# Attention's output projection in three fp32r passes, its weights through the split ring

## The reference, cut to what matters

```python
o = diff_attention(q, k, v, lam, rel_bias)            # 4 heads x 128
o = rms_norm(o, subln[l], SUBLN_EPS) * (1.0 - lam_init)
y_a = o.reshape(B, S, D_ATTN) * jax.nn.silu(z_a)      # 512 x 512
...
m = jax.nn.sigmoid(g_a) * (y_a @ w_pa[l]) + jax.nn.sigmoid(g_h) * (y_h @ w_ph[l])
x = x + rms_norm(m @ w_out[l], post_norm[l], NORM_EPS)
```

## Time and profile before

| | us |
|---|---|
| median of three runs | 2135.15 (2129.75 to 2135.77) |
| profiled execution | 2135.83 |
| its span | 2133.8 |
| TensorE busy, matmul rows | 2038.1 (96%) |
| VectorE / ScalarE / GpSimd busy | 1258.6 / 913.7 / 650.2 |
| mean granted TensorE clock | 0.972 |

### The profile page before, as it was taken

One profiled execution on the slowest core, in us unless ns is written; L12 is line 12 of the kernel. 1 busy time (PEld: TensorE's weight loads), 2 busy tenths in 40 slices (PEclk: granted clock), 3 DMA queues, 4 the chain that ended last, 5 costly groups with the idle time before them and its releaser, 6 DMA issues.

```text
span 2133.8 us, 28186 instructions
## 1 busy us (share of the span) xinstructions
PE 2038.1 (96%) x10992; PEld 1543.0 (72%) x10992; DVE 1258.6 (59%) x1994; ACT 913.7 (43%) x1458; POOL 650.2 (30%) x308
## 2 busy tenths in 40 slices
PE   8999999999999999999999998999999999989997
PEld 6667874657767775567777787777877878867776
DVE  4688945447779864465758844545134876464432
ACT  4432245333432345343357346446234743454531
POOL 2323431224324332033334212223433422222252
PEclk9999999998999999999899999899999999989998
DMA  6223221142322332132222001112332210111232
GB/s 226 84 92 116 93 90 52 68 138 79 113 99 72 107 104 69 50 119 69 104 89 80 28 27 43 50 52 93 104 117 86 89 48 15 35 60 50 66 108 84
DMA packets 47858, 174.26 MB, mean 82 GB/s; under 512 B 5646, under 2 KB 6286, under 8 KB 46320
## 3 DMA queue, kind: packets, MB, share of 16 engines
q1 hardware_dynamic: 47600, 172.34, 23.9%
q10 hardware_dynamic: 128, 0.13, 0.0%
HBM read 157.77 MB, written 14.68 MB: 81 GB/s over the span
## 4 chain that ended last, share of the span: by engine, by line
PE 73%; DVE 21%; ACT 3%; issue 2%; DMA 1%; DVEq 0%; ACTq 0%
PE bank L610 13%; PE bank L619 13%; PE bank L624 12%; PE bank L727 4%; PE bank L739 2%; PE bank L1152 2%; PE bank L1132 2%; PE bank L655 1%; PE bank L810 1%; PE bank L824 1%; PE bank L887 1%; DVE arena L1943 1%; DVE arena L1947 1%; PE bank L747 1%; DVE arena L1945 1%
## 5 line engine op out<-in xcount | busy, mean ns | idle before, releaser
L2497 POOL TENSOR_TENSOR w_lo<-wraw,w_hi 128x1024 fp32r<-128x1024 f32 (+2 forms) x248 | 591.8, 2388 | 1341.9 <-ACT w_hi L1222 1341.9
L1222 ACT ACTIVATE w_hi<-wraw 128x1024 fp32r<-128x1024 f32 (+2 forms) x248 | 253.1, 1021 | 690.2 <-PE bank L624 428.4
L610 PE MATMUL bank<-h_hi,w_hi 128*128 128x512 f32 x1568 | 409.7, 404 | 4.9 <-DVE arena L2231 3.8
L619 PE MATMUL bank<-h_lo,w_hi 128*128 128x512 f32 x1568 | 388.9, 390 | 0.2
L624 PE MATMUL bank<-h_hi,w_lo 128*128 128x512 f32 x1536 | 379.5, 389 | 0.0
L610 PEld LDWEIGHTS bank<-h_hi,w_hi 128*128 128x128 f32 x1568 | 294.1, 191 | 96.7 <-issue 31.8
L619 PEld LDWEIGHTS bank<-h_lo,w_hi 128*128 128x128 f32 x1568 | 294.7, 188 | 64.0 <-DVE h_lo L1782 1.6
L624 PEld LDWEIGHTS bank<-h_hi,w_lo 128*128 128x128 f32 x1536 | 288.3, 188 | 59.9
L727 PE MATMUL bank<-arena,wdir 128*128 128x512 f32 x256 | 114.7, 599 | 1.2 <-DMA wdir<-in_w_direct 1.2
L1979 DVE CUSTOM_DVE_ANT_0 arena<-bank,arena 128x512 f32<-128x512 f32 x64 | 44.3, 692 | 89.7 <-PE bank L810 88.4
L2403 DVE TENSOR_TENSOR bank<-bank,con 128x128 f32<-128x128 f32 x64 | 19.2, 300 | 129.4 <-PE bank L1138 128.3
(11 more groups left out here) (402 smaller groups left out, 3256.1 us busy)
## 6 DMA issues: line engine op xcount, KB each, us to landing
wraw<-in_w_split SPq DMA_DIRECT2D x220, 512.0 KB, 3.3
wdir<-in_w_direct SPq DMA_DIRECT2D x16, 512.0 KB, 3.3
x_park<-arena SPq DMA_DIRECT2D x3, 2048.0 KB, 6.3
arena<-x_park SPq DMA_DIRECT2D x3, 2048.0 KB, 7.8
wraw<-in_w_split SPq DMA_DIRECT2D x12, 384.0 KB, 3.0
hg_park<-arena SPq DMA_DIRECT2D x2, 2048.0 KB, 8.6
arena<-hg_park SPq DMA_DIRECT2D x2, 2048.0 KB, 7.9
wraw<-in_w_split SPq DMA_DIRECT2D x16, 256.0 KB, 2.6
```

What stands on the lines that cost most here:

```text
L610: mm(ps[0:wd, 0:S], hi[:, k, :].bitcast(F32R), h_hi[:, k, :].bitcast(F32R), start=k == 0 and not begun, stop=False)
L619: ins = mm(ps[0:wd, 0:S], hi[:, k, :].bitcast(F32R), h_lo[:, k, :].bitcast(F32R), start=False, stop=bool(parts) and k == KT - 1)
L1222: a(w_hi[:, n % 2, 0:f].bitcast(F32R), wraw[:, n % 2, 0:f], ACT.Copy).then_inc(hi_done, 1)
L2497: nc.gpsimd.tensor_tensor(w_lo[:, n % 2, 0:f].bitcast(F32R), wraw[:, n % 2, 0:f], w_hi[:, n % 2, 0:f], ALU.subtract).then_inc(lo_done, 1)
```

## The change

`pa` leaves the direct path. Its name goes into `PAIRED` with four parts, so each of its four chunks of a layer (two tiles each) goes through the ring ahead of `wo`'s. The code for such a tile, which stood in the second block, becomes a function `paired_tile` for both. y_a gets a leading part `za_hi` (ScalarE, `keep_leading`, one copy of 128 x 512 for each head) and a remainder `za_lo` (VectorE, `leave_rest`). TensorE's wait for the last head gives way to a wait for each part in the first `pa` tile. ScalarE makes the leading parts of the chunks two places ahead inside the loop that makes `h_hi`. The residual is loaded in four transfers of 512 KB, each behind a weight load. `wdir` is left to `ph`. TensorE then has 96 fp32r matmuls per layer in place of 32 in fp32.

The diff, cut to what the text speaks of:

```diff
@@ -56,7 +56,7 @@
 CHUNK = KT * P
 
 
-PAIRED = {"qr": 3, "qn": 3, "kn": 2, "vv": 2}
+PAIRED = {"pa": 4, "qr": 3, "qn": 3, "kn": 2, "vv": 2}
 SPLIT = ("u", "q", "k", "v", "za", "zh", "gh", "ga", "lx", "gc", "gba", "lz", "mq", "mkv", "gz", "mz",
          "wo", "wo2")
 PARTS = {"A0": 0, "M0": 1, "A1": 2, "M1": 3, "B0": 4, "V0": 5, "B1": 6, "V1": 7}
...
@@ -174,7 +174,7 @@
 
 
     split, direct = [], []
-    per = {"pa": 2, "ph": 2}
+    per = {"ph": 2}
     for job in psum_plan():
         g, l, n = job[0], job[1], job[-1]
         if g == "wo2":
...
@@ -196,9 +196,10 @@
     for n in range(len(direct)):
         todo.append((-5 if n < 2 else at[direct[n - 2][1]] + 0.2, "direct", n))
     for l in range(DEPTH):
+        todo += [(at["pa", l, 2 * n] + 0.3, "x in", f"A{l}{n}") for n in range(4)]
         todo += [(at["flt", l, 0, 3, 1] + 0.3, "filter weights", l), (at["u", l, 9] + 0.3, "park", l),
                  (at["iy", l, 0, 3] + 0.3, "unpark", l),
-                 (at["iy", l, 1, 3] + 0.3, "bias", l), (at["os", l, H - 1] + 0.3, "x in", f"A{l}"),
+                 (at["iy", l, 1, 3] + 0.3, "bias", l),
                  (at["ps", l] + 0.3, "x out", f"A{l}"), (at["mo", l, MH - 1] + 0.4, "x in", f"B{l}")]
         if l:
             todo += [(at["os", l - 1, H - 1] + 0.4, "layer", l), (at["wo2", l - 1, KT - 1] + 0.3, "x out", f"B{l - 1}")]
...
@@ -370,6 +375,10 @@
         lu, lr, li, la, lbb = (view(rb, n, 4, S) for n in ("lt", "XT", "X", "qg", "at"))
         lw = arena[:, rb["spare"]:rb["spare"] + 512].rearrange("p (g j c) -> p g j c", g=2, j=4)
         row_q = rs[:, :]
+        with early:
+            za_lo, za_hi = (typed(name, at, 4 * S)[:, :].rearrange("p (k s) -> p k s", k=4) for name, at in
+                                   (("za_lo", ra["za"]), ("za_hi", rt["WT"] + 4 * S)))
+        early_tiles[0], typed_to[0] = False, 0
         oa_rest = typed("oa_rest", rb["oa"], 4 * S).rearrange("p (h s) -> p h s", h=4)
         oc_rest = typed("oc_rest", rb["oc"], 4 * S).rearrange("p (h s) -> p h s", h=4)
         parts_at = typed("kr_parts", rb["mq"], 3 * S)
...
@@ -551,14 +560,17 @@
                 elif kind == "x in":
                     l = int(n[1])
                     if n[0] == "A":
+                        k = slice(2 * int(n[2]), 2 * int(n[2]) + 2)
                         sp.wait_ge(*after("ya", l, H - 1))
+                        if l:
+                            sp.wait_ge(x_out, 16 * l)
+                            sp.dma_start(xs["A1"][:, k, :], t["x_park"][:, k, :]).then_inc(x_in, 16)
+                        else:
+                            sp.dma_start(xs["A1"][:, k, :], t["xT"].rearrange("(k p) s -> p k s", p=P)[:, k, :]).then_inc(x_in, 16)
                     else:
                         sp.wait_ge(*full("mo", l, MH - 1))
-                    if n == "A0":
-                        sp.dma_start(xs["A1"], t["xT"].rearrange("(k p) s -> p k s", p=P)).then_inc(x_in, 16)
-                    else:
                         sp.wait_ge(x_out, 16 * NORMS[n])
-                        sp.dma_start(xs["B1"] if n[0] == "B" else xs[n], t["x_park"]).then_inc(x_in, 16)
+                        sp.dma_start(xs["B1"], t["x_park"]).then_inc(x_in, 16)
                 elif kind == "x out":
                     l = int(n[1])
                     if n[0] == "A":
...
@@ -625,6 +637,27 @@
                                  stop=k == KT - 1)
                 ins.then_inc(filled(*job), 1)
 
+            def paired_tile(g, l, j, src_hi, src_lo, made):
+
+                kt = PAIRED[g]
+                n = SPLIT_AT[g, l, j - j % 2]
+                hi, lo = (part[:, n % 2, 0:2 * kt * P].rearrange("p (j k n) -> p j k n", j=2, k=kt)[:, j % 2, :, :]
+                          for part in (w_hi, w_lo))
+                ps = take(g, l, j)
+                pe.wait_ge(hi_done, n + 1)
+                for k in range(kt):
+                    if made:
+                        pe.wait_ge(*after(f"{made}_hi", l, k))
+                    mm(ps[:, 0:S], hi[:, k, :].bitcast(F32R), src_hi[:, k, :].bitcast(F32R), start=k == 0, stop=False)
+                pe.wait_ge(lo_done, n + 1)
+                for k in range(kt):
+                    mm(ps[:, 0:S], lo[:, k, :].bitcast(F32R), src_hi[:, k, :].bitcast(F32R), start=False, stop=False)
+                for k in range(kt):
+                    if made:
+                        pe.wait_ge(*after(f"{made}_lo", l, k))
+                    ins = mm(ps[:, 0:S], hi[:, k, :].bitcast(F32R), src_lo[:, k, :].bitcast(F32R), start=False, stop=k == kt - 1)
+                ins.then_inc(filled(g, l, j), 1)
+
             def split_pair(first, second, parts):
 
                 n = SPLIT_AT[first]
...
@@ -720,7 +753,10 @@
                     if g in SPLIT:
                         split_tile(g, l, j)
                         return
-                    per, kt, src = {"pa": (2, 4, za), "ph": (2, 4, uc)}[g]
+                    if g == "pa":
+                        paired_tile(g, l, j, za_hi, za_lo, "za" if j == 0 else None)
+                        return
+                    per, kt, src = 2, 4, uc
                     ps = take(g, l, j)
                     w = direct_w((g, l, j - j % per), kt)
                     for k in range(kt):
...
@@ -846,7 +882,6 @@
                     column_sums(("os", l, h), [(tmp[:, h % 2, :], ("o_sq", l, h))])
                 for j in BEFORE_HEAD_NORM[H]:
                     tile("ga", j)
-                pe.wait_ge(*after("ya", l, H - 1))
                 for j in range(KT):
                     tile("pa", j)
                 for j in range(KT):
...
@@ -874,25 +909,8 @@
                     if g in SPLIT:
                         split_tile(*((g, l) if j is None else (g, l, j)))
                         return
-                    kt = PAIRED[g]
...
+                    paired_tile(g, l, j, src_hi, src_lo, made if j == 0 and g != "qn" else None)
...
@@ -1443,6 +1461,9 @@
                         for half in range(2):
                             gates_ = PH[:, 4 * half:4 * half + 4, :]
                             a(gates_, gates_, ACT.Sigmoid).then_inc(up("gh_sig", l, half), 1)
+                def keep_leading(h):
+                    a(za_hi[:, h, :].bitcast(F32R), za[:, h, :], ACT.Copy).then_inc(up("za_hi", l, h), 1)
+
                 keep("ga", 1)
                 keep_values(H - 1)
                 for h in range(H):
...
@@ -1456,12 +1477,21 @@
                     if h:
                         act.wait_ge(*after("ya", l, h - 1))
                     root(("os", l, h), P, EPS5)
+                    if h:
+                        keep_leading(h - 1)
                 for j in BEFORE_HEAD_NORM[H]:
                     keep("ga", j)
+                act.wait_ge(*after("ya", l, H - 1))
+                keep_leading(H - 1)
                 for half in range(2):
                     gates_ = PA[:, 4 * half:4 * half + 4, :]
                     a(gates_, gates_, ACT.Sigmoid).then_inc(up("ga_sig", l, half), 1)
-                parts_hi(f"M{l}", PA, lambda k: after("gated", l, k))
+
+                def gated(k):
+                    await_split("pa", l, k)
+                    return after("gated", l, k)
+
+                parts_hi(f"M{l}", PA, gated)
                 for j in range(KT):
                     if j == KT - 1:
                         load_roots()
...
@@ -2009,6 +2039,11 @@
                         dve.wait_ge(*full("ph", l, j))
                         dve.wait_ge(*after("gh_sig", l, j // 4))
                         v.tensor_tensor(PH[:, j, :], bank("ph", l, j)[:, 0:S], PH[:, j, :], ALU.mult).then_inc(release("ph", l, j), 1)
+                def leave_rest(h):
+                    dve.wait_ge(*after("za_hi", l, h))
+                    v.tensor_tensor(za_lo[:, h, :].bitcast(F32R), za[:, h, :], za_hi[:, h, :],
+                                    ALU.subtract).then_inc(up("za_lo", l, h), 1)
+
                 for h in range(H):
                     dve.wait_ge(*read("os", l, h))
                     dve.wait_ge(*read("za", l, h))
...
@@ -2017,6 +2052,9 @@
                                                     ALU.mult))
                     v.tensor_tensor(za[:, h, :], za[:, h, :], oA[:, h, :], ALU.mult).then_inc(up("ya", l, h), 1)
                     dve.wait_ge(*after("ya", l, h))
+                    if h:
+                        leave_rest(h - 1)
+                leave_rest(H - 1)
                 for j in range(KT):
                     dve.wait_ge(*full("pa", l, j))
                     dve.wait_ge(*after("ga_sig", l, j // 4))
...
@@ -2025,7 +2063,7 @@
                     dve.wait_ge(*read("ph", l, j))
                     v.tensor_tensor(PA[:, j, :], PA[:, j, :], PH[:, j, :], ALU.add).then_inc(up("gated", l, j), 1)
                 lo_odd(f"M{l}", PA)
-                dve.wait_ge(x_in, 16 * (l + 1))
+                dve.wait_ge(x_in, 64 * (l + 1))
                 for j in range(KT):
                     dve.wait_ge(*full("wo", l, j))
```

28 lines of the change are left out of this document (7 added, 21 removed).

## The result

| | before | after |
|---|---|---|
| median, 9 runs each | 2135.8 us (2129.75 to 2137.43) | 2141.12 us (2140.22 to 2141.66) |
| ratio, 95% interval | | 1.0024 [1.0015, 1.0033] |
| profiled execution, its span | 2135.83, 2133.8 | 2141.27, 2139.4 |
| mean granted clock of that execution | 0.972 | 0.968 |

The forecast was 2139.6 with a range of 2131 to 2146. The change costs a quarter of a per cent: a slowdown, but one inside the 0.3% that the prediction had called no change.

What follows compares the result with a forecast made beforehand. TensorE's own stream and its waits were taken as the bound. To the profiled 2135.83 it added 0.8 (layer 1 +1.1, layer 0 -0.35) and 3.6 for the clock, giving 2140.2; the median being 0.7 lower, 2139.6 us, range 2131 to 2146.

Steps and rivals of the forecast that it cites:

- F: When VectorE sees the last `pa` result, 0.27 us after `pa` leaves TensorE; put at T + 23.9.
- T: Start of `pa` on TensorE in each layer; 437.89 in layer 0 and 938.38 in layer 1 before the change.
- The passes and the start: In `pa`: fp32r passes gain 12.0 us over both layers; a first-tile wait for the last head costs 1.8 per layer.
- The ring: Weight chunks and residual during `pa`: no cost; layer 0's third chunk has 3.5 us cover, at worst costs 1.5.
- The first `wo` tile: GpSimd's four even remainders wait behind the second chunk's split, 1.71 us each; second `wo` tile starts at T + 34.9.
- The clock: Gaps between matmul pairs in the first `wo` tile halve TensorE's clock behind them: 1.8 us per layer, 3.6 in all.
- The sign, 0.50 in the tile behind: Evidence to look for: a granted clock of 0.50 in the tile behind the four waits for remainders.
- Rival A: The clock holds through the matmul pairs of the first `wo` tile; time 2136 us, chance 0.22.
- Rival C: The 1.8 us wait at the start of `pa` drops the clock too, 3.3 us per layer; 2146 us, chance 0.15.
- B: Rival: remainders in the first `wo` tile are not late, second tile at T + 29.9; 2126 us, chance 0.08.

Runs made afterwards that it cites:

- a2: Changed kernel, with ScalarE making the last head's leading part ahead of the last `ga` tile's two instructions; 2138.84 us, ratio 1.0012.
- a3: Changed kernel with the edits of a1 and a2 together; 2131.87 us, ratio 0.9975.
- c1: Changed kernel with a2's edit, and the gated sum's remainders on GpSimd and VectorE spread through `pa` instead of in a block; 2130.21 us, ratio 0.9962.
- c3: Changed kernel with a2's edit, and all eight gated-sum remainders on VectorE, GpSimd left with the weight splits; 2127.4 us, ratio 0.9962.
- c4: a3, with TensorE running the second `wo` tile's first pass between the first tile's second and third passes; 2125.16 us, ratio 0.9952.
- a1: Changed kernel, with GpSimd's four even remainders one chunk earlier, ahead of the split of the second `wo` chunk; 2132.14 us, ratio 0.9985.
- a5: Changed kernel, with VectorE's four odd remainders for `wo` cut from 512 to 8 columns, the rest left uncomputed; 2135.47 us, ratio 0.9999.
- a4: Changed kernel, with four needless matmuls ahead of each pair in the first `wo` tile's third pass, waits kept; 2137.31 us, ratio 1.0003.

## Why the prediction was right

The mechanism, each of its places and the size of each large term held; the size of the clock's term partly by luck. By its steps, from the profiled executions:

| step | predicted | measured |
|---|---|---|
| 96 matmuls of `pa` | 21.8 | 22.09 |
| wait in the first `pa` tile | 1.8 | 1.83 (942.98 - 940.47 - 0.68) |
| F | T + 23.9 | T + 24.12 (964.59) |
| split of the second `wo` chunk ends | F + 3.7 | F + 3.7 (968.26) |
| four even remainders end | F + 10.5 | F + 10.45 (975.04) |
| second `wo` tile, full clock | T + 34.9 | T + 35.1 |
| clock, both layers | 3.6 | 3.69 |
| everything else | 0 | +0.8 |

**The passes and the start.** Both right. An fp32r matmul took 0.230 in passes of four (22.09 / 96), a little over the 0.227 of the earlier trace rows. That is what made F 0.2 late; the 0.27 from the last matmul to VectorE stood in no row, and was 0.20 (964.39 to 964.59). The copy of the last head stood behind the two instructions named, as ScalarE's rows show:

```profile
940.72 1.06 ACT L1240 ACTIVATE w_hi<-wraw 128x1024 fp32r<-128x1024 f32 x1 [3.94 <-issue]
941.68 0.58 ACT L1322 ACTIVATE arena<-bank 128x512 f32<-128x512 f32 x1
942.29 0.63 ACT L1465 ACTIVATE za_hi<-arena 128x512 fp32r<-128x512 f32 x1
```

**The ring.** TensorE waited for no chunk, as said, but the reason given was wrong. The cover of 3.5 us for the third chunk in layer 0 was worked out with a landing of 3.3 us and without GpSimd's part of the split. The small loads of the next layer, some 1 MB, had gone out in the 4 us ahead of it, the chunk landed 6.0 us after its issue, and ScalarE waited 1.61 for it:

```profile
446.68 1.06 ACT L1240 ACTIVATE w_hi<-wraw 128x1024 fp32r<-128x1024 f32 x1 [1.61 <-DMA wraw<-in_w_split]
```

GpSimd then split it from 447.82 to 450.23, and TensorE's second pass of the fifth tile wanted that at 437.07 + 1.83 + 13 x 0.92 = 450.9. The cover was 0.7 us, and it existed only thanks to the 1.8 us at the start; a2, a3, c1, c3 and c4, which have no start wait, all wait there for 0.93 to 1.12. A median of a transfer is taken from a queue that is mostly quiet; behind a burst it isn't the number to use.

**The first `wo` tile.** Right in every part: the order of waits, 1.71 us for a remainder (four took 6.83) and GpSimd's turn coming first. a1 shows that GpSimd's order was the decisive wait, and a5 that 1.71 is 1.27 plus the hold-off. The Trainium skill, "SBUF — State Buffer", section "Who interferes with whom", says that a VectorE operation with at most one SBUF input, outside the two-port modes, stays out of the contention with GpSimd, and that one with two does not when GpSimd reads SBUF; c1's rows agree, 0.68 for the one and 2.18 for the other beside the same GpSimd instruction.

**The clock.** The two lengths at 0.50 that the earlier trace rows show, 3.3 and 6.7 us, both came: the longer in layer 0, the shorter in layer 1, each partly inside the waits, where it costs nothing. The cost of 3.6 was a choice between 3.4 and 6.8 that was not worked out, so it is partly luck that 3.69 was measured; a2's execution has the longer one in both layers. The sign, 0.50 in the tile behind, was too strong: the level was 0.50 for the first 3.4 us of the second tile in layer 0 and the first 1.8 in layer 1. Rival A, that the clock holds, is refuted by 0.76 and 0.85 over the second tiles; a4 shows that it is the gaps that do it. Rival C, that the wait of 1.8 us at the start drops the clock too, is refuted by 1.00 over the whole of `pa` in both layers. But its condition was not a good one, as the last section shows.

**B**, that the remainders are not late, is refuted by four waits. It is what c4 comes nearest to: with 2125.16 it reaches B's 2126, by an edit to TensorE's order.

The profiled execution came out 1.1 us above the sum (2141.27 against 2140.2). The start of the second tile accounts for 0.4 of that, the clock for 0.1, and the untouched stretches for the rest. The medians of the nine runs each are 5.3 apart, where the forecast says 4.4.

Three expectations of the experiments did worse than the prediction. a1, a3 and c1 were to be 4 to 7 us faster than they were, above all for one reason: I moved GpSimd's instructions and costed VectorE's at their undisturbed 0.69. The late third chunk in layer 0 (a3, c1) and the clock behind the waits that stayed are the rest. In c3 the rival, which lets the two engines share their time, came within 1 us and the theory, which did not, missed by 3.4. c4, whose fill does not depend on it, came out as expected, but for the third chunk in layer 0.
